# Head norms, rotation, gates and transposes moved beside the input projections of a four-layer network on one core

## The reference, cut to what matters

```python
# even mixer (first block, layer 0): u = h @ w_in, 3328 columns, for 512 latent and 256 context tokens
q_lat = apply_rope(attn_q_heads(p['a_q'], qk_g[0]), cos, sin)   # rms_norm over 64 columns, gain, rotation
k_lat = apply_rope(kv_heads(p['a_k'], qk_g[1]), cos, sin)
a_lat = window_attention(q_lat, k_lat, kv_heads(p['a_v']), k_ctx, v_ctx, sink)   # local attention
...
def gates(f_raw):
    f = lb + (1.0 - lb) * jax.nn.sigmoid(to_heads(f_raw, HGRN_HEADS).astype(F32))
    return 1.0 - f, jnp.log(f)
q_l = jax.nn.silu(to_heads(p['b_q'], HGRN_HEADS).astype(F32))
o_fw, _ = gla_chunked(q_l, k_fw, i_l, lf_fw, s_fw)              # gated scan: 4 heads x 2 directions = 8 runs
o_bw, _ = gla_chunked(flip(q_l), flip(k_bw), flip(i_l), flip(lf_bw), s_bw)
b_lat = gated_head_norm(o_fw + flip(o_bw), p['b_g'], out_g)
...
# second block, per layer: gates of the delta rule, 24 columns of the input projection
g_f = -exp(A_log[0]) * softplus(a_f + dt_bias[0])               # and g_b
beta_f = jax.nn.sigmoid(b_f.astype(f32))                        # and beta_b
gc = jnp.cumsum(g, over a chunk);  exp(gc), exp(gc[-1] - gc), exp(gc[-1])
```

## Time and profile before

| | us |
|---|---|
| median of 3 runs (range) | 4082.05 (4080.58 to 4082.73) |
| the profiled execution | 4088.78 |
| its span | 4087.0 |
| PE busy in the span | 3805.1 (93%) |
| DVE busy | 2240.8 (55%) |
| ACT busy | 1530.3 (37%) |
| POOL busy | 341.6 (8%) |
| mean granted clock of PE, as a share of full speed | 0.947 |

### The profile page before, as it was taken

The page is one execution under the profiler, slowest core; times in us unless marked ns, Lnnn a source line. Parts: engine busy times, 40 slices in busy tenths (PEclk is TensorE's granted clock), DMA queues, the critical chain, the costliest instruction groups (busy, mean ns, idle before and its releaser), DMA issues. The chain is left out here.

```text
span 4087.0 us, 49821 instructions
## 1 busy us (share of the span) xinstructions
PE 3805.1 (93%) x20537; PEld 3114.3 (76%) x20537; DVE 2240.8 (55%) x3209; ACT 1530.3 (37%) x2348; POOL 341.6 (8%) x292
## 2 busy tenths in 40 slices
PE   7998789999999999999999979989998979988998
PEld 4884567888887888878877758757787757867886
DVE  5724765545465444572266756544477856544375
ACT  2114632111354322352254335433365335533264
POOL 0000220000000000000000045200000034400000
PEclk9997879999999999999999979979999979988999
DMA  5510012333212121123222100022222200012231
GB/s 199 176 42 10 6 42 81 126 124 129 69 61 75 64 66 60 62 76 100 92 96 91 58 12 1 1 83 78 94 96 83 68 12 1 1 63 76 88 103 62
DMA packets 254721, 288.91 MB, mean 71 GB/s; under 512 B 6756, under 2 KB 226939, under 8 KB 254517
## 3 DMA queue, kind: packets, MB, share of 16 engines
q1 hardware_dynamic: 252437, 281.84, 21.4%
q10 hardware_dynamic: 2080, 4.19, 0.3%
HBM read 283.92 MB, written 2.10 MB: 70 GB/s over the span
## 5 line engine op out<-in xcount | busy, mean ns | idle before, releaser
L476 PE MATMUL banks<-h_halves,w_halves 128*128 128x512 f32 (+1 forms) x3728 | 1391.9, 373 | 56.3 <-DVE h_halves L264 32.4
L477 PE MATMUL banks<-h_halves,w_halves 128*128 128x512 f32 (+1 forms) x3728 | 1387.2, 372 | 0.0
L478 PE MATMUL banks<-h_halves,w_halves 128*128 128x512 f32 (+1 forms) x3728 | 1380.4, 370 | 0.0
L476 PEld LDWEIGHTS banks<-h_halves,w_halves 128*128 128x128 f32 x3728 | 713.5, 191 | 196.4 <-issue 49.4
L478 PEld LDWEIGHTS banks<-h_halves,w_halves 128*128 128x128 f32 x3728 | 711.5, 191 | 122.3
L477 PEld LDWEIGHTS banks<-h_halves,w_halves 128*128 128x128 f32 x3728 | 713.5, 191 | 117.6 <-issue 0.5
L264 DVE TENSOR_TENSOR w_halves<-work,w_halves 128x2048 fp32r<-128x2048 f32 (+1 forms) x212 | 481.3, 2270 | 434.8 <-ACT w_halves L259 434.5
L259 ACT ACTIVATE w_halves<-work 128x2048 fp32r<-128x2048 f32 (+1 forms) x212 | 401.4, 1894 | 409.0 <-PE banks L478 388.6
L259 ACT ACTIVATE h_halves<-kept 128x512 fp32r<-128x512 f32 (+1 forms) x520 | 332.1, 666 | 301.4 <-PE banks L478 231.5
L264 DVE TENSOR_TENSOR h_halves<-kept,h_halves 128x512 fp32r<-128x512 f32 (+1 forms) x520 | 360.8, 736 | 133.0 <-ACT h_halves L259 132.3
L1016 DVE SCALAR_TENSOR_TENSOR kept<-kept 128x512 f32<-128x512 f32 x280 | 188.2, 744 | 7.2 <-DMA kept<-in_mod_w 7.2
(11 more groups left out here) (388 smaller groups left out, 4973.7 us busy)
## 6 DMA issues: line engine op xcount, KB each, us to landing
work<-in_w_ff SPq DMA_DIRECT2D x64, 1024.0 KB, 5.3
work<-in_ffn_w_in SPq DMA_DIRECT2D x44, 1024.0 KB, 5.1
kept<-in_mod_w SPq DMA_DIRECT2D x40, 1024.0 KB, 5.1
work<-in_odd_w_in SPq DMA_DIRECT2D x24, 1024.0 KB, 5.4
work<-in_w_in SPq DMA_DIRECT2D x24, 1024.0 KB, 5.0
work<-in_ffn_w_out SPq DMA_DIRECT2D x16, 1024.0 KB, 5.2
work<-in_even_w_in SPq DMA_DIRECT2D x13, 1024.0 KB, 5.1
work<-in_odd_w_out SPq DMA_DIRECT2D x8, 1024.0 KB, 5.1
```

The costliest lines, as they stand in the source:

```text
L476: nc.tensor.matmul(o, low[:, k - a, fc], rh[:, tc], start=(k == 0), stop=False)
L477: nc.tensor.matmul(o, high[:, k - a, fc], rl[:, tc], start=False, stop=False)
L478: mm = nc.tensor.matmul(o, high[:, k - a, fc], rh[:, tc], start=False, stop=(k == K - 1))
```

## The change

1. **The projection's finish.** `EvenCopy` takes the place of `Copy`: ACT evacuates everything, three instructions of 512 columns per group, and applies Silu or Sigmoid there. The context columns of both tiles share one bank (`packed`), which frees banks 6 and 7.
2. **Norm and rotation of queries and keys beside the projection.** `QueriesKeys` is the new side object and wraps `Modulation`. A second call in each group, `tensor_late`, comes after k = 6, and POOL and SP get parts too. The rotation is made by copies of 32 partitions by transfer and three POOL operations per tile, where it was a matmul; the duplicated keys are made by transfers. The stages `head_norm` "qk" and `rope_stage` are gone.
3. **Transposes.** The value tile of the attention and the four value tiles of the gated scan are transposed by PE beside the groups 9, 11 and 12, and ACT copies them.
4. **The first run of the gated scan** (`GlaPlan`) is prepared inside `window_stage`: its tables, one logarithm, the sum, differences, exponentials and products. `gla_stage` begins with the first scores; the other three logarithms follow the exponentials of the second run.
5. **Second block, each layer.** The gates move into `Convolutions`, in groups 8 to 12. `turn_stage` keeps the 24 transposes, with the copies shared by DVE and ACT, and takes the loads and the cast that opened `mixer_stage`.

The core of the diff:

```diff
+class EvenCopy(Finish):
+    FUNC = {3: ACT.Silu, 4: ACT.Silu, 5: ACT.Sigmoid, 6: ACT.Sigmoid, 7: ACT.Sigmoid, 8: ACT.Sigmoid, 11: ACT.Silu,
+            12: ACT.Silu}
...
+            nc.scalar.activation(core.u(2 * g + f)[:, LAT], banks[0], func).then_inc(free, 1)
+            if f == 1:
+                o = core.sb(U0 + 2 * g * T, 2 * T).rearrange("p (f t) -> p f t", t=T)[:, :, 0:CTX]
+                nc.scalar.activation(o, core.ps[:, 4 + j % 2, :].rearrange("p (f t) -> p f t", t=CTX), func).then_inc(free, 2)
...
+class QueriesKeys:
+    SQUARES = {1: (0, 1), 2: (2, 3), 3: (4,)}
+    SPREADS, SPREADS_LATE = {6: 0, 7: 2, 8: 4}, {6: 1, 7: 3}
+    COPIES = {6: (0, 1), 7: (2, 3), 8: (4,)}
+    HEADS = {11: (0, 1), 12: (2, 3)}
...
+    def load(self, sp, at):
...
+        if at == 9:
+            sp.wait_ge(self.scaled, self.N)
+            sp.dma_start(self.cos, core.const("cosA")).then_inc(self.tables_in, 16)
+            sp.dma_start(self.sin, core.const("sinA")).then_inc(self.tables_in, 16)
+            self.swap(sp, 0)
+            self.swap(sp, 1)
+        if at == 10:
+            for m in range(2, self.N):
+                sp.wait_ge(self.roped, m - 1)
+                self.swap(sp, m)
...
+    def sums(self, pe, m):
+        nc.tensor.matmul(core.ps[0:self.ROWS, 6, :], place, self.sq[m % 2][:, LAT], start=(m == 0), stop=(m == self.N - 1))
...
+    def spreads(self, pe, m):
+        if m == 0:
+            pe.wait_ge(self.rstd_done, 1)
+            pe.wait_ge(self.table_in, 16)
+        else:
+            pe.wait_ge(self.copied, 2 * m)
+        pick = core.sb(self.table + m * P, P, self.ROWS)
+        nc.tensor.matmul(core.ps[:, 6, :], pick, self.std[:, LAT], start=True, stop=True)
...
+    def turn(self, pe, src):
+        for t in range(6):
+            mm = self.nc.tensor.transpose(core.ps[:, 6 + t // 4, (t % 4) * P:(t % 4 + 1) * P], src[:, t * P:(t + 1) * P],
+                                          core.ident())
...
+    def gpsimd(self, pool):
+        for m, x in enumerate(self.tiles):
+            pool.wait_ge(self.copied, 2 * m + 2)
+            nc.gpsimd.tensor_tensor(x, x, self.back, ALU.mult).then_inc(self.scaled, 1)
...
+            nc.gpsimd.tensor_tensor(x[:, LAT], x[:, LAT], self.cos, ALU.mult).then_inc(self.turned, 1)
+            nc.gpsimd.tensor_tensor(o, o, self.sin, ALU.mult).then_inc(self.turned, 1)
+            pool.wait_ge(self.turned, 2 * m + 2)
+            nc.gpsimd.tensor_tensor(x[:, LAT], x[:, LAT], o, ALU.add).then_inc(self.roped, 1)
...
+class GlaPlan:
+    def scalar(self, act, s):
+        if s == 2:
+            self.logs(0).then_inc(self.lf_done, 1)
+        if s == 7:
+            nc.scalar.activation(self.DEC[0], self.ch3(self.CU)[:, :, self.at_end[0]], ACT.Exp)
+            nc.scalar.activation(self.QS[0], self.CU, ACT.Exp).then_inc(self.e_done, 1)
+        if s == 9:
+            self.key(0).then_inc(self.kk_done, 1)
...
+    def vector(self, dve, s):
+        if s == 5:
+            self.scan(0).then_inc(self.cum_done, 1)
...
 class Convolutions:
+        if at == 9:
+            act.wait_ge(self.gate_pe, 1)
+            nc.scalar.activation(self.v4(pl.beta), self.gates()[:, :, 0:12], ACT.Sigmoid).then_inc(self.gate_act, 1)
...
+        if j == 10:
+            pe.wait_ge(self.centred, 2)
+            pe.wait_ge(self.gate_dve, 5)
...
+        if j == 11:
+            pe.wait_ge(self.gate_act, 5)
...
+def turn_stage(core, nc, a, l, pl):
...
+            for b in range(1, 6, 2):
+                act.wait_ge(turned, b + 1)
+                nc.scalar.activation(dst(b), bank(b), ACT.Copy)
...
+            pool.wait_ge(loads_in, 16 * 6)
+            nc.gpsimd.tensor_copy(pl.dist16, pl.dist)
```

More of the change, by code:

```diff
@@ L474, in group @@
                                     tc = slice(t0, t0 + tw)
[L475 to L478, removed]
+                                    o, shared = banks(j, f)[s], self.packed and s == 1
+                                    opens = k == 0 and not (shared and f == 1)
+                                    nc.tensor.matmul(o, low[:, k - a, fc], rh[:, tc], start=opens, stop=False,
+                                                     skip_group_check=shared)
+                                    nc.tensor.matmul(o, high[:, k - a, fc], rl[:, tc], start=False, stop=False,
+                                                     skip_group_check=shared)
+                                    mm = nc.tensor.matmul(o, high[:, k - a, fc], rh[:, tc], start=False, stop=(k == K - 1),
+                                                          skip_group_check=shared)
                                 if k == K - 1:
@@ L488, in group @@
                                 side.tensor(pe, i * B + j)
+                            if side is not None and k == 6:
+                                side.tensor_late(pe, i * B + j)
                 def group_tile(j, k):
@@ L537, in _ @@
                     group(G // B, j)
-            if before is not None:
-                block.gpsimd(before.gpsimd)
+            @block.gpsimd
+            def _(pool):
+                if before is not None:
+                    before.gpsimd(pool)
+                if side is not None:
+                    side.gpsimd(pool)
             def wait_tile(eng, i, n):
@@ L645, in takes @@
         return True, True
[L648 to L656, removed]
-            nc.scalar.activation(core.sb(self.where(g, f) + lo, w), banks[0], ACT.Copy).then_inc(free, 1)
-        def vector(dve, g, j, f, banks, free, gates):
-            lo, w = segs[1]
-            nc.vector.tensor_copy(core.sb(self.where(g, f) + lo, w), banks[1]).then_inc(free, 1)
-        self.scalar = scalar
-        self.vector = vector if len(segs) == 2 else None
 class ResidualSum(Finish):
@@ L963, in __init__ @@
         self.slots, self.sums, self.halves_at = slots, sums, halves_at
-        self.before = None
+        self.before, self.opens = None, False
     def take(self, sems, free):
@@ L2516 @@
     SEMS = 22
+    LOADS = 16 * 5
     PAD = CONV_K // 2
@@ L2806, in _ @@
-            chain.wait()
-            nc.vector.tensor_tensor(pl.ekd, core.ps[:, 7, 48:96], pl.gsum, ALU.subtract).then_inc(sums, 1)
-            dve.wait_ge(chain_a, 2)
-            nc.vector.scalar_tensor_tensor(out=pl.nbge, in0=pl.beta, scalar=-1.0, in1=pl.eg, op0=ALU.mult, op1=ALU.mult)
+            for b in range(0, 6, 2):
+                dve.wait_ge(turned, b + 1)
+                nc.vector.tensor_copy(dst(b), bank(b))
         @block.scalar
         def _(act):
-            act.wait_ge(turned, 1)
@@ L3498, in second_layer @@
     cat = (0, 1, 4, 5, 6, 19, 20, 21)
-    into.run(f"in2_{l}", before=before, side=Convolutions(core, nc, l))
     pl = DeltaPlan(core)
-    delta_gates_stage(core, nc, a, l, pl)
+    into.run(f"in2_{l}", before=before, side=Convolutions(core, nc, l, a, pl))
+    turn_stage(core, nc, a, l, pl)
     mixer_stage(core, nc, a, l, pl)
```

633 lines of the change are left out of this document (382 added, 251 removed).

## The result

| | before | after |
|---|---|---|
| median (range), three runs each | 4082.05 (4080.58 to 4082.73) | 4033.39 (4031.48 to 4045.78) |
| ratio, 95% interval | | 0.989 (0.986 to 0.992) |
| profiled execution | 4088.78 | 4033.39 |
| mean granted clock | 0.947 | 0.954 |
| median of all runs of this study | 4082.5 (32 runs, 4074.7 to 4088.9) | 4035.2 (9 runs, 4025.8 to 4045.8) |

The changed kernel is 48.7 us faster by the first medians and 47.3 by all runs; the forecast was 4034. L... are lines of the changed kernel from here on, and in the experiments those of each run's own kernel. First the busy time by stage, columns as in the earlier trace rows: the even projection, local attention, the opening of the gated scan up to the masked scores of run 1, the rest of the scan.

The account below looks back on a forecast made before the run. PE bounds the even projection, latency the norm and rotation, a tight ring local attention, DVE the gated scan; -51.7 + 20.0 + 9 - 14.2 - 11.2 = -48.1 gives a median of 4034.0 us, range 4015 to 4058.

Parts of the forecast that it names:

- A: Between even projection and local attention: the stages of norm and rotation are removed, -51.7 us.
- B: Beside the even projection: added PE work, 17.7 us at full clock, 2.3 expected for a slow stretch, +20.0 us.
- the relay over POOL, SP and ACT: Beside the even projection: these engines' part in preparing queries and keys, rotation done some 40 us before the end.
- Rival 4: Even projection: engines' relay ends late, PE waits for the last heads in group 12; 4054 us, chance 0.06.
- rival 2: Even projection's clock drops behind every spread (27 us), and local attention pays 17.7 us in full; 4050 us, chance 0.11.
- Rival 3: Even projection: low clock persists through groups 5 to 9, 84 us more; 4118 us, slower than before, chance 0.03.
- C: Local attention: it takes on the preparation of the gated scan's first run, +9 us (0 to 17.7).
- Rival 1: Local attention absorbs the added work near 0, and the second block gains 11.6 us a layer; 4019 us, chance 0.12.
- guests: Local attention: the gated scan's preparation work placed there, including a logarithm with table loads, 4.2 us in one step.
- the ring: Local attention: its tightly coupled engines, PE, ACT and DVE, with gaps of under 1 us at most places.
- D: Gated scan's opening: run 1's masked scores begin after 16.7 us instead of 30.9, -14.2 us (-18.6 to -11).
- E: Second block: gates' stage -4.2 us, mixer's start -4.2, input projection +2.8; -5.6 a layer, -11.2 in all.

Follow-up runs that it names:

- the second trace: The changed kernel run again with no edit: median 4041.72 us (4025.76 to 4044.52), ratio 0.988; its profiled run took 4044.52.
- run 6: Not a follow-up run of the study: one of the numbered runs inside the gated scan, a part of each kernel's execution; no time of its own is given.
- second trace of before: The kernel before run once more, unedited, for a further trace: 4081.48 us.
- third of the changed kernel: The changed kernel run once more, unedited, for its trace alone: 4035.22 us.

## Why the prediction was right

**Where it read rows, it hit.** A and B together, -31.7, measured -31.8. The sums cost what the rows of before gave (1.43 each for 1.42), PE never waited for the relay over POOL, SP and ACT, and the rotation was done 46 us before the end (40 forecast). That held although two of POOL's scalings took 6.50 and 5.94 us, where the forecast had 2.1 at worst. Rival 4 is out.

**B's clock term was right in kind.** Four spreads one by one were followed by no slow stretch, the one behind the reductions cost 2.0 (2.3 charged). Where the slow stretches fall is not fixed, though. In the second trace group 3 kept its clock (21.96 us, 23.50 in the first) and group 7 took 28.32 instead of 26.78; from group 1 to group 8 all three traces took 147.3. Doubling the spreads cost 17.4 us where their own time is 7.1, so the condition "one by one, between dense products" carried that estimate; with it gone, rival 2's price would have been too small. Rival 3 is out.

**C was right in sum, its parts shifted.** +9.0 against +9, +8.7 over the three traces. The logarithm with its loads cost 5.1 to 5.9 rather than 4.2, the other parts 3 to 4 rather than 4.8. Rival 1's first half, that attention has room, is refuted by attention at 96.7 us without guests, and rival 2's second half, that the ring pays 17.7, by the same 9.1.

**D was right in size, but one step of it failed.** The opening took 16.0 us for 16.7, so run 1's masked scores gained 14.9. The forecast then said that nothing later gives this back. Something did: run 2's masked scores came 28.06 us into the scan, 40.62 before, which is 12.6. Between the two, DVE's timeline in the changed kernel has these rows:

```profile
460.52 2.59 DVE L2197 TENSOR_TENSOR work<-work,kept 128x768 f32<-128x768 f32 x1
...
465.33 0.29 DVE L2225 COPY work<-banks 128x128 f32<-128x128 f32 x1 [0.55 <-PE banks L2272]
...
469.65 1.21 DVE L2210 COPY_PREDICATED work<-work,banks 64x384 f32<-64x384 uint32 x2 [0.20 <-PE banks L2259]
```

The same product takes 0.94 in the trace before; here POOL's product began 0.04 us ahead of it (460.48, 1.81 us). With the two waits for PE that is 1.65 + 0.55 + 0.20 = 2.4 us, the 14.9 less 12.6. From run 4 to run 6 the gain is a steady 13.3. The rest of the first pair's 16.4 lies behind the last masked scores, where 10.9 us in the trace before stand against 8.4 after. In the second trace of before this end took 8.4 too, and in the second and third of the changed kernel 10.4 and 10.5. So that part can't be credited to the change, and over all traces the scan gained 13.2 for 14.2.

**E was right per layer in the first pair.** -5.9 and -5.6 for -5.6: POOL's wait for the sixth load set the end of the stage of the transposes, as forecast, and the mixer's first scores came at 4.8 for 5.9. Over all traces it is -5.8 and -4.2, since to its last scores the last mixer took 2.0 us longer in the changed kernel's second trace, and 1.0 less in that of before.

**What the forecast left out** is the chance of the clock. The 55.4 us between the first profiles are 50.8 of the touched stretches (48.1 forecast) and 8.7 of the mixers' tails, less 4.1 elsewhere; over all traces the touched stretches give 46.7. The forecast took its sum from the profiled execution and then moved it to the median by 6.7 us, which kept this out of the number. The second trace of before, at 4081.48, is 7.3 us shorter than the first, 3.1 of it in the scan and 3.4 in the last mixer, both run by the same instructions.

**How much was luck.** The sum is borne out: 46.7 to 50.8 for 48.1. That the first median hit 4034.0 within 0.6 us is luck: the next five runs of the same kernel had their median at 4041.72, and all nine span 20 us (those of before 14), where the forecast had three runs within 2.2. A single run could have missed by 10.

## What to carry to other kernels

Work moved beside a PE-bound projection cost little more than its PE time (1.67 us for a spread of 1.42) where each sparse product stood alone between dense ones; two in a row were followed by the lower clock in four pairs of five, and with it five doubled spreads cost 17.4 us for 7.1. A tight ring of engines may have no room even where its engines wait a third of the time. The guest that came in one piece of 4.2 us cost all of it and more (5.1 to 5.9); the small ones, 3.8 us of ACT's time and 7.4 of DVE's, cost 3 to 4. Compare a guest with a stage of its own. One trace of each kernel is not enough for an account by stage: a stretch that the change doesn't touch differed by 5 us between two traces of one kernel. When a stage shrinks, look at what it waits for next: here the loads issued inside the stage of the transposes were worth some 13 us in the traces (11 in the medians), about what the change had won in that block (11.5).

## What the runs showed of the hardware that was not expected

- PE was busy without a gap in the groups of the even projection, and still the granted clock fell to 0.50 in places: behind reductions of 3.86 us (behind those of group 3 in two of the changed kernel's three traces) and behind two spreads in a row (2.8 us), but not behind reductions of 1.84 us, one spread (1.4 us) or two sums in a row (2.9 us, 128 rows in). The Trainium skill ("TensorE: Matmul & The Clock Gate", Part 1) puts the clock down to how busy PE has been; the records count such products as busy, so by them the rule doesn't tell these cases apart.
- The same program takes 4025.8 to 4044.5 us in five runs on one chip. In the last mixer's tail alone 79 equal records take 18.2 or 22.9 us.
- POOL's product of 128x768 takes 1.84 us alone, but 6.50 and 5.94 beside a row of DVE's two-input multiply-adds, as its timeline shows. Both times its record ends 1.7 us after the row does (213.11 against 211.44, 237.77 against 236.06): as if it had stood still until the row was over, and not taken turns with it. PE waited for none of this.

```profile
206.61 6.50 POOL L1235 TENSOR_TENSOR kept<-kept 128x768 f32<-128x768 f32 x1 [124.21 <-ACT kept L1152]
214.58 1.84 POOL L1235 TENSOR_TENSOR kept<-kept 128x768 f32<-128x768 f32 x1 [1.48 <-ACT kept L1152]
```
